# A peer-routed expert block: the query product on x times the norm's weights, the token factor and the shift applied to the scores, the first head routed ahead, the output product two abreast

## What is computed

```python
x = x + gate1 * (y @ w_out)
h2 = _rmsnorm(x, norm2_g) * (1.0 + scale2) + shift2
# _peer(h2, ...):
q = (h2 @ w_q).reshape(B, S, 8, 256)                 # 8 heads, two halves of 128
s1 = einsum(q[..., :128], sub_keys_1); s2 = einsum(q[..., 128:], sub_keys_2)
v1, i1 = top_k(s1, 16); v2, i2 = top_k(s2, 16)       # 16 of 128 keys for each half
best, ci = top_k(v1[..., :, None] + v2[..., None, :], 16)
expert_idx = i1[ci // 16] * 128 + i2[ci % 16]; gates = softmax(best)
out = sum over heads and the 16 of gelu(h2 . expert_u[idx]) * gates * expert_v[idx]
```

## Time and profile before

| | us |
|---|---|
| median of 3 runs (lowest, highest) | 1496.72 (1495.39, 1499.38) |
| the profiled execution's own time | 1496.53 |
| its span in the profile | 1494.8 |
| mean granted TensorE clock, share of full | 0.96 |
| PE, DVE, ACT, POOL busy | 1256.0, 1077.9, 612.8, 278.7 |
| moved by DMA | 417.09 MB, 268.45 MB of them gathers |

### The profile page before, as it was taken

How to read it: one execution, slowest core, us unless ns; L and a number is a source line. 1 busy time by engine, 2 the same in 40 slices (tenths; PEclk the granted TensorE clock), 3 DMA queues, 4 the chain that set the end, 5 groups by cost and what they waited for, 6 DMA issues and landing times. The chain is left out here.

```text
span 1494.8 us, 19530 instructions
## 1 busy us (share of the span) xinstructions
PE 1256.0 (84%) x6980; PEld 941.3 (63%) x6980; DVE 1077.9 (72%) x2178; ACT 612.8 (41%) x1247; POOL 278.7 (19%) x278
## 2 busy tenths in 40 slices
PE   1987999998788977777777777777599989999997
PEld 1987999998783322323223222323289978999997
DVE  6569656565769867777777677776489977898646
ACT  2444645454614333333332233333363244544445
POOL 0000000000144543434334343433000000000000
PEclk8799999999999999999999999999799999999999
DMA  9376633254397999999999999999725343554450
GB/s 384 125 265 254 262 137 137 89 176 160 134 412 313 421 421 421 421 421 421 421 421 421 420 421 421 421 421 422 322 104 186 141 169 125 185 198 152 166 218 29
DMA packets 55517, 417.09 MB, mean 279 GB/s; under 512 B 6016, under 2 KB 7680, under 8 KB 8976
## 3 DMA queue, kind: packets, MB, share of 16 engines
q0 software_dynamic: 36864, 268.45, 43.3%
q1 hardware_dynamic: 18112, 146.71, 26.7%
q10 hardware_dynamic: 464, 0.88, 0.2%
HBM read 414.97 MB, written 1.05 MB: 278 GB/s over the span
## 5 line engine op out<-in xcount | busy, mean ns | idle before, releaser
L936 PE MATMUL ps<-arena 128*128 128x512 f32 x512 | 240.7, 617 | 80.5 <-ACT arena L1340 80.5
L936 PE MATMUL ps<-ring,arena 128*128 128x512 f32 x448 | 216.3, 630 | 49.2 <-ACT arena L1340 49.1
L936 PEld LDWEIGHTS ps<-arena 128*128 128x128 f32 x512 | 95.2, 194 | 224.4 <-ACT arena L1340 118.2
L1930 DVE CUSTOM_DVE_ANT_0 arena<-arena 128x1024 f32<-128x1024 f32 x128 | 151.6, 1223 | 112.9 <-DMA arena<-in_experts,rowid 111.3
L554 POOL DMA_INDIRECT arena<-in_experts,rowid x128 | 133.0, 1039 | 399.7 <-DVE rowid L1904 221.4
L630 PE MATMUL ps<-h_hi,w_hi 128*128 128x256 f32 x704 | 199.9, 284 | 5.9 <-DVE h_lo L1550 3.6
L631 PE MATMUL ps<-h_hi,w_lo 128*128 128x256 f32 x704 | 198.0, 281 | 0.0
L632 PE MATMUL ps<-h_lo,w_hi 128*128 128x256 f32 x704 | 198.0, 281 | 0.0
L936 PEld LDWEIGHTS ps<-ring,arena 128*128 128x128 f32 x448 | 85.6, 199 | 177.9 <-issue 93.2
L1333 ACT ACTIVATE arena<-arena 128x2 f32<-128x2 f32 x128 | 26.0, 203 | 398.5 <-DVE arena L1930 398.3
L630 PE MATMUL ps<-n_hi,e_hi 128*128 128x256 f32 (+1 forms) x512 | 155.1, 303 | 28.7 <-DVE n_lo L1550 17.2
(11 more groups left out here) (329 smaller groups left out, 2469.3 us busy)
## 6 DMA issues: line engine op xcount, KB each, us to landing
ring<-in_early_w SPq DMA_DIRECT2D x47, 1024.0 KB, 5.0
arena<-in_ada_w SPq DMA_DIRECT2D x24, 1024.0 KB, 5.8
arena<-in_up_w SPq DMA_DIRECT2D x11, 2048.0 KB, 8.2
arena<-in_z_w SPq DMA_DIRECT2D x9, 2048.0 KB, 8.8
arena<-in_down_w SPq DMA_DIRECT2D x8, 1408.0 KB, 6.1
arena<-in_o_w SPq DMA_DIRECT2D x2, 2048.0 KB, 8.2
arena<-in_pg_w SPq DMA_DIRECT2D x2, 2048.0 KB, 8.0
arena<-in_experts,rowid POOLq DMA_INDIRECT x128
```

Of the source, the lines that this page charges most:

```text
L936: mm = pe.matmul(BK[4 + 2 * t + b], diag[:, j, :], rows[j][:, D + b * 512:D + (b + 1) * 512], start=first and j == 0, stop=last and j == E ...
L1930: v.tensor_tensor_reduce(out=u, in0=u, in1=h2tok[:, t, :], scale=1.0, scalar=0.0, op0=ALU.mult, op1=ALU.add, accum_out=dots[:, even, j:j + ...
```

## The change

The norm of x is a factor r[t] for each token: h2 = r[t] * x[t] * w + shift, with w = (1 + scale2) * norm2_g. So q = r[t] * ((x * w) @ w_q) + shift @ w_q, and the scores follow as r[t] times the scores of the first term plus the scores of the second, which are the same for all tokens.

- The activation of pq becomes x * w, split as `x2_hi` and `x2_lo`, with two more columns that hold the shift (258 columns for 256). It needs no norm.
- `norm2_sums` takes the place of `add_two`: it stands inside the first pq pair after k = 3, and also makes the sums with tokens on partitions by four one-column products. ACT makes both inverse roots; the small one lies in `csil`.
- `head_scores` has two more fp32 matmuls, the shift's query broadcast over 128 columns, into bank 3; ACT copies them (`copy_shifted`); DVE makes the scores by one multiply-add for each tile in place of one copy of both. `scores` now counts 16.
- pq uses banks 0 to 2. `head_scores(0)` moves from after pq block 2 into its middle.
- wo starts two abreast in place of four. The splits of weights at the bb and wo blocks move (after DVE's blocks 0, 1, 3, 5 of bb; before 2, 4, 6 of wo).
- DVE takes tile 0 of head 0's scores and routes it before anything else; the rest of its list is written anew, with the first two pairs of dot products of head 0 ahead of the last scores.

The diff, cut to its core (index changes of semaphore counts, views and the constant halves left out):

```diff
 def banks():
+        if key[0] == "pq":
+            b = key[1] % 3
@@ tensor
+            def norm2_sums():
+                pe.wait_ge(S("n2_sum"), KD - 2)
+                pe.wait_ge(S("n2_sq"), KD)
+                two = (0, KD - 1)
+                for k in two:
+                    pe.matmul(BK[4][:, 0:T], ones[:, :], hT[:, k, :], start=k == 0, stop=k == KD - 1,
+                              skip_group_check=True)
+                for t in range(NT):
+                    for k in two:
+                        mm = pe.matmul(BK[5][:, t:t + 1], hT[:, k, t * P:(t + 1) * P], ones[:, 0:1],
+                                       start=k == 0, stop=k == KD - 1, skip_group_check=True)
+                mm.then_inc(S("norm_ss"), 1)
...
-            abreast("wo", 4, m_hi, m_lo, "wo")
-            for b in range(4, 8):
+            abreast("wo", 2, m_hi, m_lo, "wo")
+            for b in range(2, 8):
                 product_parted(("wo", b), m_hi, m_lo)
-            add_two("n2", 4, "norm_ss")
             def head_scores(h):
+                if h == 0:
+                    pe.wait_ge(S("norm_std"), norm_count("n2"))
...
                 pe.wait_ge(S("taken_A"), taken_by("A", BLOCK_AT[("pq", 2 * h + 1)]))
+                q = [qs[:, (2 * h + half) % 4, :] for half in range(2)]
                 for half in range(2):
-                    for t in range(NT):
+                    mm = pe.matmul(BK[3][:, (2 * (h % 2) + half) * P:(2 * (h % 2) + half + 1) * P],
+                                   q[half][:, T:T + 1].broadcast_to([P, P]), keyT[:, half, :], start=True, stop=True)
+                mm.then_inc(S("score_mm"), 1)
+                for t in range(NT):
+                    for half in range(2):
...
-            abreast("pq", 2, n_hi, h2_lo, "n2")
+            abreast("pq", 2, x2_hi, x2_lo, "n2", between=norm2_sums, after=3, n=T + 2)
             for b in range(2, 16):
-                product_parted(("pq", b), n_hi, h2_lo)
-                if b % 2 == 0:
+                product_parted(("pq", b), x2_hi, x2_lo, n=T + 2, between=(lambda: head_scores(0)) if b == 2 else None)
+                if b % 2 == 0 and b > 2:
                     head_scores(b // 2 - 1)
@@ scalar
             for b in range(8):
-                if b % 2 == 0:
+                if b in (0, 1, 3, 5):
                     part()
                 act.wait_ge(S("comb"), b + 1)
...
+            act.activation(x2_hi[:, :, T:T + 2], adaT[:, 24:32].rearrange("p (a b) -> p a b", b=1).broadcast_to([P, KD, 2]),
+                           ACT.Copy)
             for k in range(KD):
                 if k in (0, 4, 6):
                     part()
                 act.wait_ge(S("taken_V"), taken_by("V", BLOCK_AT[("wo", k)]))
-                act.activation(sq[:, k, :], xT[:, k, :], ACT.Square).then_inc(S("n2_sq"), 1)
+                act.activation(x2_hi[:, k, 0:T], xT[:, k, :], ACT.Copy, scale=mod[:, k:k + 1]).then_inc(S("x_hi"), 1)
+                act.activation(hT[:, k, :], xT[:, k, :], ACT.Square).then_inc(S("n2_sq"), 1)
             act.preload_act_table(ACT.Ln)
+            part()
             act.wait_ge(S("norm_ss"), norm_count("n2"))
-            inverse_root(stat[:, 1, :], BK[4][:, 0:T], D, "norm_std")
+            act.activation(stat[:, 1, :], BK[4][:, 0:T], ACT.Ln, scale=1.0 / D, bias=epsc[:, 0:1])
+            link(act.activation(csil[:, 0:2], BK[5][:, 0:2], ACT.Ln, scale=1.0 / D, bias=epsc[:, 0:1]))
+            act.activation(stat[:, 1, :], stat[:, 1, :], ACT.Exp, scale=-0.5)
+            act.activation(csil[:, 0:2], csil[:, 0:2], ACT.Exp, scale=-0.5).then_inc(S("norm_std"), 1)
-            for k in range(KD):
-                act.wait_ge(S("n2_scaled"), k + 1)
-                act.activation(n_hi[:, k, :], hT[:, k, :], ACT.Identity, bias=adaT[:, 24 + k:25 + k]).then_inc(S("x_hi"), 1)
-            part()
             for b in range(2):
-                take(("pq", b), qs[:, b, :])
+                take(("pq", b), qs[:, b, :], n=T + 2)
...
+            copy_shifted(0)
@@ vector
             rest()
             for b in range(8):
-                if b in (4, 6):
+                if b in (2, 4, 6):
                     rest()
                 link(stt(xT[:, b, :], arrived(("wo", b))[:, 0:T], adaT[:, 16 + b:17 + b], xT[:, b, :], ALU.mult, ALU.add),
                      "taken_V")
+                if b:
+                    lo_of_x2(b - 1)
                 if b >= 2:
-                    add_to_first("n2", b - 1)
+                    add_to_first("n2", b - 1, hT)
+            lo_of_x2(7)
             rest()
             v.wait_ge(S("norm_std"), norm_count("n2"))
             for k in range(KD):
                 stt(hT[:, k, :], xT[:, k, :], mod[:, k:k + 1], stat[:, 1, :]).then_inc(S("n2_scaled"), 1)
-                if k >= 2:
-                    lo_of_h2(k - 2)
...
-            rest()
-            scores(0)
+            scores(0, 0)
             route(0, 0)
             rest()
-            scores(1)
-            rest()
-            scores(2)
+            scores(0, 1)
+            both_scores(1)
             rest()
             soft_weights(0, 0)
-            route(1, 1)
-            scores(3)
-            rest()
-            scores(4)
-            rest()
-            scores(5)
-            scores(6)
-            scores(7)
+            top_keys(1, 0)
+            top_keys(1, 1)
+            both_scores(2)
+            rest()
+            top_pairs()
+            both_scores(3)
+            rest()
+            look_up(0)
+            look_up(1)
+            name_rows(1)
+            rest()
+            both_scores(4)
             v.wait_ge(S("h2tok"), 4)
+            dot(0, 0, 0, 0)
+            both_scores(5)
+            dot(0, 0, 0, 1)
+            both_scores(6)
+            both_scores(7)
             head(0, 0, 0, first=True)
```

More of the change, by code:

```diff
@@ L226, in two_blocks @@
         with ExitStack() as over:
-            h2_lo = over.enter_context(nc.sbuf_tensor("h2_lo", [P, KD, T], F32R))
+            x2_lo = over.enter_context(nc.sbuf_tensor("x2_lo", [P, KD, T + 2], F32R))
         sq = sb("sq", [P, KD, T])
@@ L636, in column, with abreast @@
                 return key[1] * P % CHUNKS[chunk_of(BLOCK_AT[key])][5]
-            def abreast(name, m, x_hi, x_lo, stage, between=None):
-                outs = [begin((name, b))[0][:, 0:T] for b in range(m)]
+            def abreast(name, m, x_hi, x_lo, stage, between=None, after=KD - 2, n=T):
+                outs = [begin((name, b))[0][:, 0:n] for b in range(m)]
                 for k in range(KD):
@@ L647, in abreast, with product_parted @@
                             mm.then_inc(S("product"), 1)
-                    if between and k == KD - 2:
+                    if between and k == after:
                         between()
-            def product_parted(key, x_hi, x_lo, c0=None, m=P):
+            def product_parted(key, x_hi, x_lo, c0=None, m=P, n=T, between=None):
                 bank, _ = begin(key)
                 for k in range(KD):
-                    mm = three(bank[0:m, 0:T], key, column(key) if c0 is None else c0, k, x_hi, x_lo, m)
+                    mm = three(bank[0:m, 0:n], key, column(key) if c0 is None else c0, k, x_hi, x_lo, m)
+                    if between and k == 3:
+                        between()
                 mm.then_inc(S("product"), 1)
@@ L688, in sum_all @@
                 mm.then_inc(S(summed), 1)
-            def add_two(tag, bank, summed):
-                pe.wait_ge(S(tag + "_sum"), KD - 2)
-                pe.matmul(BK[bank][:, 0:T], ones[:, :], sq[:, 0, :], start=True, stop=False, skip_group_check=True)
-                pe.wait_ge(S(tag + "_sq"), KD)
-                pe.matmul(BK[bank][:, 0:T], ones[:, :], sq[:, KD - 1, :], start=False, stop=True,
-                          skip_group_check=True).then_inc(S(summed), 1)
+            def norm2_sums():
[10 more added lines that the diff above has]
+                mm.then_inc(S("norm_ss"), 1)
             pe.wait_ge(S("ones"), 1)
@@ L938, in head @@
                         mm.then_inc(S("v_used"), 1)
-            pe.wait_ge(S("scores"), EH)
+            pe.wait_ge(S("scores"), NT * EH)
             head(0, 0, first=True)
@@ L1320, in _ @@
                 if b >= 4:
-                    act.wait_ge(S("score_mm"), b // 2 - 1)
-                take(("pq", b), qs[:, b % 4, :])
+                    act.wait_ge(S("score_mm"), 2 * (b // 2 - 1))
+                take(("pq", b), qs[:, b % 4, :], n=T + 2)
+                if b % 2 == 0 and b > 2:
+                    copy_shifted(b // 2 - 1)
+            copy_shifted(EH - 1)
             assert parted[0] == PARTED_EARLY
@@ L1935, in head @@
                 for p in range(PAIRS):
-                    dot(g, even, t, p)
+                    if not first or p >= 2:
+                        dot(g, even, t, p)
                     if p == 1:
```

54 lines of the change are left out of this document (34 added, 20 removed).

## The result

| | before | after |
|---|---|---|
| median, us (lowest, highest) | 1498.05 (1495.39, 1499.84) | 1477.78 (1474.49, 1479.42) |
| ratio, 95% interval | | 0.9863 [0.9838, 0.9889] |
| profiled execution: own time, span | 1496.53, 1494.8 | 1474.49, 1472.7 |

The changed kernel is faster by 1.4%, some 20 us. (The median before is now of four runs; the prediction's 1496.72 was of three.) The page after: its span, granted clock and DMA share in 40 slices (of 36.8 us).

The account below looks back on a forecast made before the run. Bound: a fixed 614 us DMA stream from head 1's first gather, its start set by PE's chain to the first expert pair. Terms -15.1 - 1.0 + 0.6 = -15.5 us, giving 1481.2 us, range 1476.0 to 1487.5.

Parts of the forecast that it names:

- wo at once: Output product: wo starts with the end of bb, takes 22.7 us, and ends 7.2 us earlier.
- pq 13.5 earlier: Query product: pq starts right at wo's end, without waiting for the norm, 13.5 us earlier.
- Roots, remainder, last scores: Waits in pq: 0.5 us for the norm's roots, 1.9 before pq 6, 0.6 before the last scores.
- rival (c): In pq 2, PE still waits for the norm because the roots come late: 1486.2 us, chance 0.04.
- Extra columns: Products of pq: 258 columns in place of 256 cost 0.3 us in all.
- rival (d): Products of pq: 258 columns break the pace, making the kernel slower, 1520 us at half-clock pace; chance 0.04.
- First pair: From the last scores to the first expert matmul: 2.7 us, where it was 6.23 before.
- The clock term: First expert pair at the higher clock: -1.0 us, bounds -2.0 and 0; separately +0.6 for pq's new waits.
- The first gather does not set the start: Head 0's first gather comes 11.2 us earlier, but DMA still runs dry some 5 us; PE sets the start.
- rival (a): Head 0's first gather sets the stream's start, with no DMA break: -11.2 us, 1485.5 us, chance 0.10.
- The stream and the tail unchanged: From head 1's first gather on: the stream stays 614 us and nothing after it is touched.
- the prediction's own last sign: A stream not 614 us long, or a tail not the same, would make the whole sum wrong.

Follow-up runs that it names:

- b_wo2: The kernel before with wo two abreast in place of four, the splits at their old places: 1493.12 us, ratio 0.9965.
- wo4: The changed kernel with wo four abreast again, banks 4 to 7 first: 1487.18 us, ratio 0.9907.
- normwait: The changed kernel with the norm's sums back ahead of pq and pq waiting for the inverse root: 1483.38 us, ratio 0.9906.
- best1: The changed kernel with pq 0 and 1 in banks 2 and 3 and the weight split ahead of wo 6 moved behind wo's takes: 1474.04 us, ratio 0.9847.
- banks: The changed kernel with pq blocks 0 and 1 in banks 2 and 3 instead of 0 and 1: 1478.27 us, ratio 0.9876.
- gatherlate: The changed kernel with head 0's first gather held back until pq block 7 is done: 1481.0 us, ratio 0.9889.
- best2: best1 with ACT's softmax, Gelu table and diagonals of the first two pairs ahead of the last scores: 1469.71 us, ratio 0.9808.

## Why the prediction was right, and where it was not

The forecast was 1481.2 in a range of 1476.0 to 1487.5; it was 1477.78, faster as said, 3.4 us below the forecast. As a change it was 15.5 us, and the medians differ by 20.3. In its own points, counted from the end of bb:

- *wo at once*: right, -4.9 at its start and 22.6 us long for my 22.7; 7.3 won at its end for 7.2. But it is owed to two abreast and to the moved splits alike: each alone wins 5.8 and 5.7 of it (b_wo2, wo4).
- *pq 13.5 earlier*: wrong, 10.2. **This is the step that failed**: I looked at pq's chunk, split and sums, and not at the bank of its second block, which was the bank of wo's last block, since pq has three banks. I had put 1.9 behind the fourth step for the same cause, DVE's late takes; it stood ahead of the first, at 3.48, and brought the lower clock (0.69 from 370 to 375), which I had given one chance in four. The scores' end still moved 10.8 for 11.9 (11.3 with the clock's 0.6), because other terms of the sum were too large. From the start of pq to there it took 64.7 us for my 67.0: waits 2.2 for 4.9 (none for the sums and the roots), the scores 10.4 for 12.6, and against them the products 48.3 for 45.3, 1.3 of it at the slow start. That the late start was made up so nearly is luck. A `head_scores` holds TensorE for 1.25 us and not 1.6, from its first matmul to the next product:

```profile
420.56 0.37 PE L635 MATMUL ps<-x_hi,e_hi 128*128 128x258 f32 x1
...
426.38 0.60 PE L911 MATMUL ps<-keyT,arena 128*128 128x128 f32 x4
...
427.63 0.37 PE L635 MATMUL ps<-x_hi,e_hi 128*128 128x258 f32 x1
```

- *Roots, remainder, last scores*: right. No gap at the scores in pq 2 (0.5), 1.53 before pq 6 (1.9), 0.63 before the last (0.6). What a wait for the norm would have cost, though ahead of pq and not inside it as in rival (c), normwait shows.
- *Extra columns*: right that they cost next to nothing; the term of 0.3 itself is too small to be told. TensorE at the end of the last block of pq, two products 14 apart:

```profile
428.80 0.28 PE L635 MATMUL ps<-x_hi,e_hi 128*128 128x258 f32 x1
...
430.47 0.28 PE L637 MATMUL ps<-x_lo,e_hi 128*128 128x258 f32 x1
```

  1.67/14 = 0.119 us, where wo has 0.118 with 256 columns, so rival (d) is false. The 48 products from 420.56 to 426.38 above took 5.82 us, the same number of 256 columns in the kernel before 5.84:

```profile
410.78 0.36 PE L630 MATMUL ps<-n_hi,e_hi 128*128 128x256 f32 x1
...
416.62 1.05 PE L894 MATMUL ps<-keyT,arena 128*128 128x128 f32 x8
```

  The Trainium skill (TensorE: Matmul & The Clock Gate, Back-to-back issue gap) has the gap of a matmul by itself grow evenly with its columns, with no step at 256. The trace agrees that there is no step. Both blocks take 0.121 to 0.122 us for one matmul, more than the 0.118 that the sum took from wo, before and after alike.
- *First pair*: 2.57 for 2.7 at the gap. The clock term was mis-sized: the granted clock was 1.00 in 435 to 445, and from the first expert matmul to the gather it took 4.5 for 6.5, so -2.0, the bound, where I took half. That it held is in part luck: behind a gap of the same 2.57 it held in five profiles (4.4 to 4.5 us to the gather) and fell in two, best1 and normwait (6.0 and 6.1).
- *The first gather does not set the start*: right, but by less than I said. It moved 9.5 for 11.2 (the bank's wait stands ahead of it; in banks it moved 12.1), and its issue took 2.87 us. From 395 to 440 the DMA share is 1.01, so it was the volume since that gather, and not the gathers gated by pq blocks, that set when head 0's data had landed, and the dry spell was 1.9 us for "some 5". gatherlate shows that the limit of rival (a) lay just behind.
- Together the first gather of head 1 came 16.4 us earlier, for 15.5: misses of opposite sign (the scores' end 0.5 too late, the first pair 1.0 and its gap 0.1 better, and smaller ones) that nearly cancelled.
- *The stream and the tail unchanged*: the stream's length held (614 us at 420 GB/s), yet from its first gather to z it took 1.6 us more than before, and 1.2 to 2.6 more in every variant of the changed kernel but gatherlate (5.7), which no run explains. The tail was not the same: -4.7 in the profiled pair, where I had taken 0. By the prediction's own last sign this speaks against the sum as a whole: it is right for the chain, and silent on the rest. In the profiled pair the tail and the earlier end of bb (2.5), more than the change's own chain (0.9), are why the time lies below the forecast; for the medians this is argued, since only profiled executions show their parts.

## What to carry to other kernels

When a product is freed from one wait, list every other resource that its first instruction takes, the PSUM bank's last reader among them, before counting its new start. Blocks computed side by side may start hardly later (1.5 us here), but all of them end late: what hangs on their results (takes, norms, splits) is delayed with their number, and this can outweigh the start. And after a gain on one chain look at how far the next limit lies: here the DMA volume lay 2 us behind, and best2 could bring the first gather of head 1 forward by 6.1 us only because its first gather of head 0 comes 5.3 us earlier too.

## What was unexpected of the hardware

- At the same granted clock of 1.00 the same matmuls of 256 columns started 0.113, 0.118 or 0.123 us apart, steady over stretches of 20 us. Two executions of one program differed in it, and their second block by 8 us.
- Whether the clock falls behind a short gap differs between executions of one program. Ahead of pq 6 the kernel before waits 3.30 us in its first profile and 3.31 in its second; the clock held in the first and fell in the second:

```profile
400.00:410.00 10.00, 6.70 (x57) 6.46 (x56) 8.99 (x18) 3.16 (x4) 4.67 (x2) 1.00 0.45 139
```

```profile
400.00:410.00 10.00, 7.14 (x47) 7.14 (x48) 6.98 (x7) 2.60 (x6) 7.88 (x5) 0.83 0.79 287
```

  A gap of 2.57 kept it in the changed kernel and lost it in best1 and normwait; one of 2.28 lost it in the kernel before. The length of a gap alone does not tell.
- Issuing a gather takes GpSimd 0.94 us, but 2.87 at 393.07, beside DVE's split of two SBUF tensors:

```profile
392.69 2.29 DVE L1624 TENSOR_TENSOR e_lo<-ring,e_hi 128x2048 fp32r<-128x2048 f32 x1
```

  The Trainium skill (SBUF — State Buffer, Who interferes with whom) has a VectorE instruction with two inputs in SBUF contend with a GpSimd instruction that reads SBUF, as a gather reads its row numbers, and the one that comes second wait until the first is through. The trace agrees: this issue began 0.38 us after the split, is longer by 1.93, and ends 0.96 after the split does; the next one, which began at 396.25, ahead of the next split (396.44), took 0.94.
